# Folding h into the gathered expert rows of a hybrid encoder step, with four places for down weights

## The reference, cut to what matters

```python
h  = x + mixed                                   # mixed: concat(SSD, conv, attention, S5) @ W_out
hn = rmsnorm(h, g_ffn)                           # 1088 rows
grp = argmax(hn @ w_group); top 2 of 8 experts of that group by hn @ w_expert
gate = softmax(top 2 logits) * softmax(group logits)[grp]
for each expert e and its tokens:
    out = (silu(hn @ w_gate[e]) * (hn @ w_up[e])) @ w_down[e]    # 1024 -> 512 -> 1024
h = h + gate0 * out0 + gate1 * out1              # the token's two experts
y = rmsnorm(h, g_final)
```

## Time and profile before

| | us |
|---|---|
| three runs | 1187.05, 1175.76, 1182.9; median 1182.9 |
| profiled execution, its own time | 1188.38 |
| span of that execution, first to last instruction | 1186.5 |
| granted TensorE clock, mean | 0.965 of full speed |

### The profile page before, as it was taken

How to read it: one execution, slowest core, us unless ns; L and a number is a source line. 1 busy time by engine, 2 the same in 40 slices (tenths; PEclk the granted TensorE clock), 3 DMA queues, 4 the chain that set the end, 5 groups by cost and what they waited for, 6 DMA issues and landing times.

```text
span 1186.5 us, 17459 instructions
## 1 busy us (share of the span) xinstructions
PE 1103.2 (93%) x7006; PEld 538.5 (45%) x7006; DVE 442.5 (37%) x1051; ACT 250.1 (21%) x489; POOL 113.8 (10%) x202
## 2 busy tenths in 40 slices
PE   7999999999998999999999999989999998988645
PEld 4666665767754654555453333333333332322211
DVE  4799989360177743232541101110011010100107
ACT  4300112113544853221210000000000000000017
POOL 0000000000072000000410010001001000100015
PEclk9999999999997989998979999999999999999968
DMA  8121123013003021103959999999999999999758
GB/s 310 50 84 38 55 67 44 1 42 96 20 2 147 1 110 73 41 20 136 363 179 342 414 416 356 411 414 416 387 413 399 414 413 412 413 412 414 315 202 323
DMA packets 73778, 271.84 MB, mean 229 GB/s; under 512 B 10784, under 2 KB 15712, under 8 KB 65632
## 3 DMA queue, kind: packets, MB, share of 16 engines
q1 hardware_dynamic: 67200, 252.47, 55.4%
q0 software_dynamic: 6048, 17.83, 3.9%
q10 hardware_dynamic: 448, 0.40, 0.1%
HBM read 251.18 MB, written 23.55 MB: 232 GB/s over the span
## 4 chain that ended last, share of the span: by engine, by line
PE 60%; DVE 17%; DMA 8%; SPq 7%; ACT 4%; issue 3%; POOL 0%; POOLq 0%; ACTq 0%; DVEq 0%
PE psA L1157 17%; PE psB L1186 9%; DVE psC L1716 7%; SPq L579 6%; PE psA L1007 5%; PE psB L1007 4%; DMA arena<-in_w_up 3%; PE psA L684 3%; PE psC L808 3%; PE psB L684 2%; DMA arena<-in_w_down 2%; PE psA L827 2%; PE psC L1142 1%; DMA arena<-hn_rows,ints 1%; DVE arena L1716 1%
## 5 line engine op out<-in xcount | busy, mean ns | idle before, releaser
L1157 PE MATMUL psA<-arena 128*32 128x512 f32 x2688 | 299.8, 601 | 23.8 <-DMA arena<-in_w_up 22.0
L1157 PEld LDWEIGHTS psA<-arena 128*32 128x32 f32 x2688 | 87.4, 111 | 218.5 <-issue 215.3
L1186 PE MATMUL psB<-arena 128*32 128x512 f32 x1344 | 152.0, 602 | 8.6 <-DMA arena<-in_w_down 8.6
L2165 DVE TENSOR_TENSOR arena<-psA,arena 128x512 f32<-128x512 f32 x21 | 14.5, 692 | 321.2 <-ACT arena L1531 321.2
L684 PE MATMUL psA<-arena 128*128 128x360 f32 (+1 forms) x384 | 120.8, 474 | 7.9 <-DVE arena L1590 7.9
L684 PE MATMUL psB<-arena 128*128 128x360 f32 (+1 forms) x384 | 118.9, 468 | 0.0
L684 PEld LDWEIGHTS psA<-arena 128*128 128x128 f32 x384 | 73.4, 192 | 52.1 <-DMA arena<-in_w_cm 7.9
L684 PEld LDWEIGHTS psB<-arena 128*128 128x128 f32 x384 | 72.8, 190 | 43.5 <-issue 0.5
L1716 DVE SCALAR_TENSOR_TENSOR psC<-arena,params,psC 128x1024 f32<-128x1024 f32 x70 | 89.9, 1284 | 0.0
L1186 PEld LDWEIGHTS psB<-arena 128*32 128x32 f32 x1344 | 42.7, 111 | 102.1 <-issue 99.7
L1531 ACT ACTIVATE arena<-psA 128x512 f32<-128x512 f32 x21 | 12.5, 597 | 311.4 <-PE psA L1157 311.4
(11 more groups left out here) (438 smaller groups left out, 1191.4 us busy)
## 6 DMA issues: line engine op xcount, KB each, us to landing
arena<-in_w_gate SPq DMA_DIRECT2D x128, 512.0 KB, 13.2
arena<-in_w_up SPq DMA_DIRECT2D x128, 512.0 KB, 16.3
arena<-in_w_down SPq DMA_DIRECT2D x64, 1024.0 KB, 15.3
arena<-expert_rows SPq DMA_DIRECT2D x16, 512.0 KB, 10.0
arena<-in_w_cm SPq DMA_DIRECT2D x15, 512.0 KB, 3.5
arena<-in_xT SPq DMA_DIRECT2D x8, 544.0 KB, 8.5
arena<-in_w_out SPq DMA_DIRECT2D x1, 4096.0 KB, 12.7
arena<-in_x_rows SPq DMA_DIRECT2D x8, 512.0 KB, 7.4
```

The costliest lines, as they stand in the source:

```text
L1157: mm = te.matmul(psA[tile, at:at + FF], xgT[:, k, tile], w[o % RG][:, k, :], start=(k == 0), stop=(k == KT - 1))
L1186: mm = te.matmul(psB[tile, n * 512:(n + 1) * 512], hT[:, k * P + c * TW:k * P + c * TW + TW], w, start=(k == 0), stop=(k == 3))
```

## The change

- POOL gathers, beside each quad's rows, two numbers per slot, `scales` = (2 x gate, root mean square of h), from a new DRAM table `gates_and_rms` that DVE and ACT write in quad 0 (`gates()` moves from quad 1 to quad 0). Since gathered row x root mean square = h, ACT makes h in the output buffer (`rows_scaled`), and DVE adds 2 x gate x result to it (`rows_added`). What is scattered is h + 2 x gate x result; the two rows of a token add up to twice the final h, and the last norm uses 4 x eps.
- `xg` gets three buffers (a gathered row is needed until its quad's result), `orow` keeps one; POOL's order becomes scatter(q), scales(q+2), gather(q+3).
- h isn't kept in SBUF: arena2 holds two more places for down weights (RD = 4) and one `xg` buffer. Four downs are loaded in the h stage instead of two. `hn` goes to DRAM from ACT's queue.
- Gate and up come as half a matrix to a part (one DMA of 1 MB, 8 KB per partition in one piece), gate first, and Silu begins when gate is done.
- The final stage is DVE add, ACT square and root, DVE reciprocal and multiply; PE, POOL and ACT's scaling drop out.
- The order of the experts is a new one.

```diff
-VISIT = [7, 26, 27, 12, 13, 20, 1, 3, 24, 10, 28, 8, 18, 0, 9, 14, 21, 2, 17, 5, 25, 19, 6, 31, 15, 4, 11, 30, 22, 23,
-         16, 29]
+VISIT = [26, 16, 8, 29, 24, 18, 14, 21, 9, 7, 31, 1, 3, 13, 23, 17, 10, 22, 6, 12, 2, 20, 0, 28, 27, 15, 25, 19,
+         5, 4, 30, 11]
-RG, RD, GC, DC = 3, 2, 4, 2
+RG, RD, GC, DC = 3, 4, 4, 2
+GU_PART = [(m, slice(h * 2 * KT // GC, (h + 1) * 2 * KT // GC)) for m in range(2) for h in range(GC // 2)]
...
-        wd = [a3.take(4 * D).rearrange("p (k n) -> p k n", k=4) for _ in range(RD)]
+        wd = [a3.take(4 * D).rearrange("p (k n) -> p k n", k=4) for _ in range(2)]
+        wd += [arena2[:, n * 4 * D:(n + 1) * 4 * D].rearrange("p (k n) -> p k n", k=4) for n in range(2)]
...
-        orow = [m4.take(D) for _ in range(2)]
+        orow = m4.take(D)
+        xg = [xg0, m4.take(D), arena2[:, (NT - 1) * D:NT * D]]
...
             def gate_up_in(n, e, c):
                 if n >= RG:
                     sp.wait_ge(m_gu, GC * LAST_Q[n - RG] + c + 1)
-                r, ks = n % RG, slice(c * GK, c * GK + GK)
-                for w, src in ((wg[r], a["w_gate"]), (wu[r], a["w_up"])):
-                    sp.dma_start(w[:, ks, :], ...).then_inc(s_wgu[r][c], 16)
+                r, (m, ks) = n % RG, GU_PART[c]
+                w, src = ((wg[r], a["w_gate"]), (wu[r], a["w_up"]))[m]
+                sp.dma_start(w[:, ks, :], ...).then_inc(s_wgu[r][c], 16)
             def down_in(n, e, c):
-                if n == E - 1:
-                    sp.wait_ge(m_gu, GC * LAST_Q[E - 3] + GC)
-                elif n >= 2 * RD:
+                if n >= RD + 2:
                     sp.wait_ge(m_dn, DC * LAST_Q[n - RD] + c + 1)
                 elif n >= RD:
-                    sp.wait_ge(m_dn, DC * LAST_Q[RD - 1] + DC)
+                    sp.wait_ge(m_dn, DC * LAST_Q[1] + DC)
...
             def activated(q):
-                ac.wait_ge(m_gu, GC * (q + 1))
+                ac.wait_ge(m_gu, GC * q + GC // 2)
...
-            def result_moved(q):
-                ...
-                ac.copy(orow[q % 2][:, 0:512], psB[:, 0:512]).then_inc(m_dnA, 1)
+            def rows_scaled(q):
+                ac.wait_ge(s_tab, 16 * (q + 1))
+                if q:
+                    ac.wait_ge(s_os, 16 * q)
+                ac.activation(orow, xg[q % 3], ACT.Identity, scale=scales[q % 2][:, 1:2]).then_inc(m_dnA, 1)
...
                 product_moved(q)
+                if q == 0:
+                    ac.wait_ge(rt_dve, RT["table"])
+                    ac.dma_start(tab_dram..., gate_table...).then_inc(s_hst[0], 16)
...
-            def result_half(q):
-                ...
-                ve.tensor_copy(orow[q % 2][:, 512:1024], psB[:, 512:1024]).then_inc(m_dnD, 1)
+            def rows_added(q):
+                ve.wait_ge(m_dn, DC * (q + 1))
+                ve.wait_ge(m_dnA, q + 1)
+                ve.scalar_tensor_tensor(out=orow, in0=psB[:, 0:D], scalar=scales[q % 2][:, 0:1], in1=orow,
+                                        op0=ALU.mult, op1=ALU.add).then_inc(m_dnD, 1)
...
             def gather(q):
-                if q:
-                    po.wait_ge(m_xt, q)
-                po.indirect_dma_start(xg, None, hn_dram, ...).then_inc(s_xg, 16)
+                if q in (1, 2):
+                    po.wait_ge(m_xt, q)
+                elif q:
+                    po.wait_ge(m_dnD, q - 2)
+                po.indirect_dma_start(xg[q % 3], None, hn_dram, ...).then_inc(s_xg, 16)
+            def gather_scales(q):
+                if q:
+                    po.wait_ge(s_tab, 16 * q)
+                else:
+                    po.wait_ge(s_hst[0], 16 * 7)
+                if q >= 2:
+                    po.wait_ge(m_dnD, q - 1)
+                po.indirect_dma_start(scales[q % 2], None, tab_dram, ...).then_inc(s_tab, 16)
             gather(0)
+            gather(1)
+            gather_scales(0)
+            gather_scales(1)
+            gather(2)
             for q in range(NQ):
-                if q + 1 < NQ:
-                    gather(q + 1)
-                if q:
-                    scatter(q - 1)
-            scatter(NQ - 1)
+                scatter(q)
+                if q + 2 < NQ:
+                    gather_scales(q + 2)
+                if q + 3 < NQ:
+                    gather(q + 3)
```

More of the change, by code:

```diff
@@ L97 @@
       "dest6": 146,
-      "dest7": 186, "slots": 197, "diag": 229, "dm": 198, "d4": 199, "spill": 206}
+      "dest7": 186, "slots": 197, "dm": 198, "d4": 199, "spill": 206, "rows": 227, "table": 234}
 class Steps:
@@ L245, in encoder_step @@
         m4 = Arena(arena4)
-        xg = m4.take(D)
+        xg0 = m4.take(D)
         xgT = m4.take(D).rearrange("p (k n) -> p k n", k=KT)
         actg, hmid, hT = (m4.take(FF) for _ in range(3))
-        orow = [m4.take(D) for _ in range(2)]
[L251 to L259, removed]
+        orow = m4.take(D)
+        xg = [xg0, m4.take(D), arena2[:, (NT - 1) * D:NT * D]]
+        FREED = E - RG
+        freed_at = 8192
+        gfin_row = freed_at // D + 4
+        gfin = arena1[:, gfin_row * D:(gfin_row + 1) * D]
+        rows = [arena1[:, n * D:(n + 1) * D] for n in range(24) if n != gfin_row]
+        og = [rows[2 * i:2 * i + 2] for i in range(NT)]
         yrow = [og[i][0] for i in range(NT)]
@@ L303, in encoder_step @@
         slotm = rt.take(BLOCKS)
+        tile_of, row_of = scaled, slotc
+        gate_table = rt.take(2 * NT * 2).rearrange("p (k i c) -> p k i c", k=2, c=2)
+        scales = [rt.take(2) for _ in range(2)]
+        eps4 = rt.take(1)
         pairs = negmask
@@ L361, in encoder_step @@
         s_xg = sem("gathered")
-        s_os = [sem(f"expert_rows{k}_out") for k in range(2)]
+        s_tab = sem("scales_gathered")
+        s_os = sem("expert_rows_out")
         s_og = [sem(f"expert_rows{i}_back") for i in range(NT)]
-        s_yo, s_gfin = sem("y_rows_out"), sem("g_final_in")
+        s_yo = sem("y_rows_out")
         zeroed = sem("zeroed_and_tail_copied")
@@ L603, in _ @@
             assert NEW[0] == [0, 1] and NEW[1][0] == 2 and LAST_Q[0] <= LAST_Q[1]
[L604 to L619, removed]
+            sp.wait_ge(rt_dve, RT["ranked"])
+            firsts = [expert(n) for n in range(4)]
+            for n in range(2):
+                for c in range(GC):
+                    gate_up_in(n, firsts[n], c)
+            sp.wait_ge(wo_pe, 4)
+            for c in range(DC):
+                down_in(0, firsts[0], c)
+            sp.wait_ge(*wo_act.at(3, "hn"))
+            for c in range(DC):
+                down_in(2, firsts[2], c)
+            sp.wait_ge(wo_pe, 8)
+            for c in range(DC):
+                down_in(1, firsts[1], c)
+            sp.wait_ge(*wo_act.at(5, "hn"))
+            down_in(3, firsts[3], 0)
             sp.wait_ge(wo_pe, NT)
@@ L1516, in _ @@
                               ).then_inc(*lg_act.of("logits"))
+                if not last:
+                    ac.wait_ge(*wo_act.at(i, "hn"))
+                    ac.dma_start(hn_dram[tok(i), :], hn[i % 2]).then_inc(s_hst[i % 2], 16)
             ac.activation(row, x, ACT.Identity, scale=hrs[:, NT - 1:NT]).then_inc(*wo_act.of("hn"))
@@ L2152, in gates @@
                 linkr(ve.tensor_tensor(gate[1], gate[0], gs, ALU.mult))
+                ve.tensor_scalar(eps4, col("eps"), 4.0, None, ALU.mult)
+                for k in range(2):
+                    ve.tensor_scalar(gate_table[:, k, :, 0], gate[k], 2.0, None, ALU.mult)
+                    last = ve.tensor_copy(gate_table[:, k, :, 1], ssum)
+                linkr(last, "table")
             def rows_moved(q):
@@ L2185, in _ @@
             ve.wait_ge(rt_pe, 6 + 2 * NT)
-            slots_out(psB[:, 1024:1024 + BLOCKS], BLOCKS, NQ)
-            ve.wait_ge(m_gu, GC * LAST_Q[E - 3] + GC)
-            for i in range(NT):
-                last = ve.tensor_scalar(gdiag[i][0:NTOK[i], 0:NTOK[i]], ident[0:NTOK[i], 0:NTOK[i]],
-                                        gate[0][0:NTOK[i], i:i + 1], None, ALU.mult)
-            linkr(last, "diag")
-            result_half(NQ - 1)
+            linkr(slots_out(psB[:, 1024:1024 + BLOCKS], BLOCKS, NQ))
+            table_rows(BLOCKS)
+            rows_added(NQ - 1)
             groups = ve.value_load(ngroups[0:1, :], min_val=0, max_val=OVG)
@@ L2339, in _ @@
+            po.wait_ge(s_os, 16 * NQ)
             groups = po.value_load(ngroups[0:1, :], min_val=0, max_val=OVG)
@@ L2356, in _ @@
             po.sem_inc(spilled, 1)
-            po.wait_ge(s_xtok[1], 16 * (NT + 1))
-            for i in range(NT):
-                po.wait_ge(f_scaled, i + 1)
-                po.tensor_tensor(og[i][1][0:NTOK[i], :], og[i][1][0:NTOK[i], :], hres[0:NTOK[i], i, :], ALU.add
-                                 ).then_inc(f_added, 1)
 _OUTS = {"y_p": (TP, D), "y_s": (TS, D), "ssd_p": (P, P), "ssd_s": (P, P), "ssd_tail": (P, 24),
```

187 lines of the change are left out of this document (89 added, 98 removed).

## The result

The changed kernel takes 1176.1 us (median of 20 runs, 1173.5 to 1182.2), the kernel before 1182.0 (median of 20). The ratio is 0.9948, with a 95% interval of 0.9927 to 0.9968: 6 us or 0.5% faster, where 5 us slower was forecast.

A forecast was written before the change was run, and what follows sets the result against it. The DMA engines were taken to bound the kernel by a little, the gathered row's chain nearly as tight. Stage +8, before it +1, final stage -4 make +5 on 1182.9: 1188 us, own range 1177 to 1200, outer 1163 to 1212.

The forecast's parts named there:

- The third gather of a quad: POOL's queue: the small table gather makes the next rows 2.7 us late in 13 of 17 quads, 35 us.
- rival A: The small gather costs no turn of the queue, so PE hardly waits for rows; 1168 us, chance 0.27.
- Rival C: Weights bound as before; waits for weights and slow clock stay near 25 us; 1177 us, chance 0.08.
- The first table: Start of the expert stage: gather(2), queued behind the first table and two scales gathers, comes 10 us late.
- Weights, lighter: Expert-stage loads: four early downs and 8 KB pieces, less the table gathers' cost, gain 20 us of DMA time.
- Waits in all: PE in the expert stage: waits and slow clock 59 us against 38, less a third of 35 + 4: +8.
- Before the stage: Ahead of the expert stage: 4.2 MB more weights run up against gather(0), +1 us (0 to 3).
- Final stage: After the last scatter: now held by loads and stores, it ends sooner, -4 us (bounds -8 and 0).

The follow-up runs named there:

- rows_first: Changed kernel with gather(2) ahead of the first two table gathers and, in every quad, gather(q+3) issued ahead of the scatter: 1163.2 us, ratio 0.9815.
- before_8kb: Kernel before with only gate and up loaded in pieces of 8 KB a row, gate ahead of up: 1179.0 us, ratio 0.9971.
- two_downs: Changed kernel with two places for down weights instead of four, no down of the third and fourth expert loaded ahead: 1184.4 us, ratio 1.0018.
- tables_two_only: Changed kernel without the table gathers after the second quad, so later quads' gates are left out: 1174.4 us, ratio 0.9919.
- tables_twice: Changed kernel with a second, useless table gather behind the first in every quad from the third on: 1178.9 us, ratio 0.996.

## Why the prediction was wrong, point by point

**The third gather of a quad** is the step that failed: "the table's two numbers 2.6 + 0.2 later". The small gather was charged a whole turn of SP's queue. Measured, it lands 0.4 to 0.7 us behind the scatter and moves the rows behind it by 0.65 to 0.7 us. A second, smaller error of the step went the same way: for the longer DVE operation the scatter was to be issued 0.6 us later, at T + 2.15, and it is issued at T + 1.63 (T + 1.55 before). The rest of the chain held: the scatter lands some 9 us after its issue, and the rows 3.8 us behind the small gather. So rows come at T + 15.1 in the median of 16 quads (14.5 to 16.0), not 17.8, and PE's want at T + 14.7 is missed by 0.4, not 3.1. The term was 35 us and measured 8.0; without any table after quad 1, the kernel is only 2 to 3 us faster. This was the mechanism of rival A, and "the 0.24 us show how near it is" was its evidence. Its 1168 missed for another reason: it is nearly the drop that the profiles show (-15 against -14.2) set against a median, while the execution of before that was profiled lay 6 us high. That the drop fits is in part luck: -12, +1 and -4 for the stage, the time ahead of it and the end were -9.6, -2.9 and -1.7.

The same holds for the forecast. From profile to profile it missed by 19 us (+5 against -14.2); that it lies only 12 us from the median is luck of the execution that was profiled before. Rival C's 1177 is the nearest number of all, by luck too: the waits that it rests on did not come.

The prediction's argument for a turn was a rule of the Trainium skill ("DMA: Bandwidth & Descriptors", Queues, rings and completion order), that an engine changes between its queues only after a whole packet. For a large gather behind a scatter the runs agree with it: it lands 3.75 us behind without a table between, and with one 0.85 us sooner when SP's DMAs for gate and up are half as long (3.59 us instead of 4.44). For a small one they don't show it: "by it a small gather costs the same turn as a large one" was the prediction's inference, and 0.65 to 0.7 us against 2.8 decides against it.

**The first table** held: the table landed at 640.0 (forecast 641), scales(0) at 646.3 (646.5), gather(2) at 657.1 (658.3), and the wait was 10.1 us (10). That it fits to 0.1 us is in part luck, as errors of about 1 us cancel: the write of the table took 5.2 us (4), gather(2) 9.2 (10.5). Taking it away gave 12 us, with the slow clock behind it. It is the dearest thing in the change, and one line removes it.

**Weights, lighter** held in its sum and was short of one part. Where hardly anything but the weights holds PE up, in rows_first, the stage lies 14 us over 482; "some 16" were forecast, though 20 off 38 are 18, and the text doesn't say how it comes to 16. Undoing the pieces costs 5 us, the two places 8 (10.2 were forecast for the loads ahead). The pieces' 8 us of DMA time are rather 10: 220 MB at 411 GB/s and at 419 differ by 10 us. But the order was counted only as a risk (rival C); it is worth 8 us. Rival C's waits of 25 us did not come: 5.8 were left.

**Waits in all**: 59 - 13 us of waits and slow clock were forecast against 38; it is 24.7 + 4.1. The third that was taken off for a queue that runs dry hid part of the error, since it was taken off a term four times too large.

**Before the stage**: +1 forecast, -2.9 in the profiles. That can't be laid to the change: quad 0 begins at 618.1 in the profile of before and at 611.0 in that of before_8kb, which differs up to there only in the pieces of the first loads; the clock granted from 553 to 618 is 0.84 in the one and 0.92 in the other. The loss that was forecast is there all the same. gather(0) landed after 4.4 us in the three kernels that load two downs ahead of the stage (before, before_8kb, two_downs) and after 5.2 to 8.4 in the eight that load four. PE waited 0.9 to 1.0 us for it in the three and 1.7 to 5.0 in the eight, one profile each: the larger load costs 1 to 4 us there, 0.8 in the profile of the changed kernel.

**Final stage**: -4 forecast, -1.7 in the profiles. The stage itself is as forecast, 37.6 us from its first load ("36 to 38") and 36.4 to 37.6 in the experiments with it, against 41.5 and 39.5 without. The rest was given back by the last scatter's landing, which the old order doesn't have (4.1 us).

Summed by the runs: pieces 5, places 8, order 8 and the final stage 2 gain, the first table takes back 12 and the others 2 to 3. That makes -8 to -9 for a measured -6; the parts were undone one at a time and overlap, so they needn't add up closer.

## What to carry to other kernels

Where a gathered operand is fetched behind the result of the same loop, work out its cycle (issue, landing, and the work up to the next issue) and set it against the loop's period: below it the operand is free, above it each microsecond counts. Then look for the wait that really guards the buffer, here the last reader of the rows and not the scatter; with the gather moved to it no wait for rows was left in the stage. A first use that needs a table just made deserves its own line in the schedule: the gather that didn't need the table was queued behind it, and that cost more than all later table gathers together.

## What the runs showed of the hardware that was not expected

- With SP's queue full of 1 MB loads, a gather of 128 rows of 8 bytes behind a scatter of the same queue delays the next large one by 0.65 to 0.7 us (tables_two_only, the changed kernel, tables_twice), and its whole transfer counts 32 packets; a gather of 128 rows of 4 KB lands 3.75 us behind a scatter of the same form (tables_two_only).
- Weights in pieces of 8 KB move at 417 to 421 GB/s in windows of 30 us from 900 to 990 in which the DMA engines are busy throughout (share 1.01 or more), in pieces of 4 KB at 411 to 413 but for one window of 397 (before, 900 to 930), in either kernel.
- A scatter of the same form and size landed after 3.7 to 4.1 us in three kernels with the old order of experts and after 4.7 to 5.7 in eight with the new one, with hardly anything else in the queues. The new one moves no more bytes (0.38 MB against 0.40). Why is open.
- A gather of 128 rows of 4 KB just ahead of the stage landed after 4.4 us in three kernels that load two downs ahead of it (4.2 MB) and after 5.2 to 8.4 in eight that load four.
